# Normalised projection input in a two-layer hybrid trunk: multiplying the last 32 projection tiles by h instead of x, and respacing the work beside them

## The reference, cut to what matters

```python
for each layer:
    x = x + 0.5 * swiglu(rmsnorm(x, norm_ffn1), ffn1_w_in, ffn1_w_out)
    h = rmsnorm(x, norm_mix)
    proj = h @ w_in                       # 6440 columns
    # columns: RWKV group (r, k, v, three small ones), short convolution (b, c, x), SSD group (z, xbc, dt)
    y_rwkv = rwkv7_mix(xs = proj + (previous_row(proj) - proj) * mu, ...)
    y_sc = rmsnorm(b_gate * causal_conv(c_gate * xt), sc_norm)
    y_ssm = mamba2_mix(z, causal_conv(xbc), dt, state, ...)
    x = x + concat([y_rwkv, y_sc, y_ssm]) @ w_out
    x = x + 0.5 * swiglu(rmsnorm(x, norm_ffn2), ffn2_w_in, ffn2_w_out)
```

## Time and profile before

| | before |
|---|---|
| median of 3 runs | 1662.56 us (1658.15 to 1662.92) |
| the profiled execution | 1660.52 us, of which its span 1658.5 us |
| mean granted clock of PE | 0.986 |
| PE busy | 1550.0 us, 93% of the span |
| DVE busy | 1145.6 us, 69% |
| ACT busy | 860.9 us, 52% |
| POOL busy | 264.0 us, 16% |
| share of PE in the chain that ended last | 19% by name; every other engine 2% or less |

### The profile page before, as it was taken

The page is one execution under the profiler, slowest core; times in us unless marked ns, Lnnn a source line. Parts: engine busy times, 40 slices in busy tenths (PEclk is TensorE's granted clock), DMA queues, the critical chain, the costliest instruction groups (busy, mean ns, idle before and its releaser), DMA issues. The chain is left out here.

```text
span 1658.5 us, 41230 instructions
## 1 busy us (share of the span) xinstructions
PE 1550.0 (93%) x17275; PEld 1471.9 (89%) x17275; DVE 1145.6 (69%) x1832; ACT 860.9 (52%) x1521; POOL 264.0 (16%) x259
## 2 busy tenths in 40 slices
PE   7999999989799899999999999998997989899997
PEld 6999999977688789999999999998775878899997
DVE  6565578795798667665575656978768977676654
ACT  5444465767444555444354444657673445554443
POOL 0000003001455531000000000030014554300000
PEclk9999999999899999999999999999998999999999
DMA  7555557471244445555454655654703453465552
GB/s 232 178 168 176 161 157 211 131 210 52 64 127 119 138 150 171 196 174 187 149 186 153 203 166 175 194 157 131 213 1 104 126 166 111 130 199 181 187 176 71
DMA packets 280649, 256.26 MB, mean 155 GB/s; under 512 B 48054, under 2 KB 268700, under 8 KB 280450
## 3 DMA queue, kind: packets, MB, share of 16 engines
q1 hardware_dynamic: 276698, 252.05, 49.3%
q10 hardware_dynamic: 3768, 1.59, 0.4%
HBM read 242.22 MB, written 11.38 MB: 153 GB/s over the span
## 5 line engine op out<-in xcount | busy, mean ns | idle before, releaser
L209 ACT ACTIVATE front_hi<-front_raw 128x1024 fp32r<-128x1024 f32 (+2 forms) x230 | 238.5, 1039 | 257.2 <-PE ps L234 249.7
L216 DVE TENSOR_TENSOR front_lo<-front_raw,front_hi 128x1024 fp32r<-128x1024 f32 (+1 forms) x210 | 252.2, 1201 | 112.5 <-ACT front_hi L209 111.7
L209 ACT ACTIVATE out_hi<-out_raw 128x1024 fp32r<-128x1024 f32 (+1 forms) x168 | 173.2, 1038 | 216.1 <-PE ps L234 202.5
L216 DVE TENSOR_TENSOR out_lo<-out_raw,out_hi 128x1024 fp32r<-128x1024 f32 (+1 forms) x148 | 183.3, 1239 | 109.9 <-ACT out_hi L209 109.3
L232 PE MATMUL ps<-front_h_hi,front_hi 128*128 128x264 f32 (+1 forms) x816 | 241.2, 296 | 8.6 <-DVE front_lo L216 6.7
L234 PE MATMUL ps<-front_h_hi,front_lo 128*128 128x264 f32 (+1 forms) x816 | 233.0, 286 | 0.0
L233 PE MATMUL ps<-front_h_lo,front_hi 128*128 128x264 f32 (+1 forms) x816 | 232.8, 285 | 0.0
L232 PE MATMUL ps<-ffn_h_hi,out_hi 128*128 128x264 f32 x704 | 200.4, 285 | 0.1
L233 PE MATMUL ps<-ffn_h_lo,out_hi 128*128 128x264 f32 x704 | 199.6, 284 | 0.0
L234 PE MATMUL ps<-ffn_h_hi,out_lo 128*128 128x264 f32 x704 | 199.6, 283 | 0.0
L232 PE MATMUL ps<-in_h_hi,front_hi 128*128 128x264 f32 x688 | 197.3, 287 | 0.0
(11 more groups left out here) (410 smaller groups left out, 3861.2 us busy)
## 6 DMA issues: line engine op xcount, KB each, us to landing
front_raw<-in_w_in SPq DMA_DIRECT2D x50, 1024.0 KB, 5.4
out_raw<-in_ffn_w_in SPq DMA_DIRECT2D x44, 1024.0 KB, 5.2
front_raw<-in_ffn_w_in SPq DMA_DIRECT2D x40, 1024.0 KB, 5.3
back_sample_rows<-row_scratch SPq DMA_DIRECT2D x160, 128.0 KB, 3.1
out_raw<-in_w_out SPq DMA_DIRECT2D x16, 1024.0 KB, 5.8
front_raw<-in_ffn_w_out SPq DMA_DIRECT2D x16, 896.0 KB, 5.0
out_raw<-in_ffn_w_out SPq DMA_DIRECT2D x16, 896.0 KB, 4.9
front_raw<-in_ffn_w_out SPq DMA_DIRECT2D x8, 1024.0 KB, 5.4
```

Of the source, the lines that this page charges most:

```text
L209: act.activation(self.hi[n % self.RING][:, 0:k, 0:w], self._raw(n), ACT.Copy).then_inc(self.hi_ready, 1)
L216: eng.tensor_tensor(self.lo[n % self.RING][:, 0:k, 0:w], self._raw(n), self.hi[n % self.RING][:, 0:k, 0:w].bitcast(F32), ALU.subtract).the ...
```

## The change

1. `NORMED = 19`. In slots 10 to 18 x·gain·rs is computed slice by slice: DVE `normed(k)` into `ctmp`, ACT `normed_hi(k)` rounds it into `h_hi`, DVE `normed_lo(k)` the rest into `h_lo`. Tiles 0 to 18 multiply the unnormalised input in other buffers; tiles 19 to 50 multiply h.
2. With h the evictions of tiles 19 to 50 need no `rs`. A `c` tile is one instruction (bank times `u`), a `b` tile multiplies `acc` by the bank (the one large instruction is gone). For the 24 late `rwkv` tiles ACT reads the bank itself, twice, and DVE adds the shifted row from the bank in one instruction, `mix_shifted`, which frees the bank; eviction and shift were two.
3. The keys now come before `b` (slots 23 to 30, `b` 31 to 34).
4. 8 low parts per layer (tiles 14, 16, 18, 20, 22, 24, 44, 46) go from POOL to DVE.
5. Decays at slots 25, 26, 28, 30 (were 25, 25, 26, 26), short convolution at 26, 27, 31, 32 (were 26, 26, 27, 27); transposes of new rows at PE slots 34, 35, 36, one bank after the other (were all at 37), their copies on ACT at 35, 36, 37; mean squares at PE slots 37 and 39; key norms one slot later; logarithm at ACT slot 45 and exponential at 46; bonus at 45, 47, 49, 50.

The core of the diff:

```diff
-                                       ("c", SC0 + 512, 0, 4), ("b", SC0, 0, 4), ("rwkv", 8 * P, 8, 8), ("rwkv", 0, 0, 8),
+                                       ("c", SC0 + 512, 0, 4), ("rwkv", 8 * P, 8, 8), ("b", SC0, 0, 4), ("rwkv", 0, 0, 8),
...
+        H, NORMED = len(tiles), 19
         ws = Stream(st, KT, pieces, halves, raw_ring=3, resident=env.first_raw, made=(env.first_hi, env.first_lo), on_dve={*range(0, base, 2), *range(1, len(halves), 2),
                                                                     *range(base + 4, base + 14, 2), *range(base + 26, base + 43, 2),
-                                                                    *range(base + 48, base + H, 2)})
+                                                                    *range(base + 12, base + H, 2)})
...
+        norm2 = Norm(st, env, "mix", lambda k: env.col("norm_mix", k), A, env.in_hi, env.in_lo, rs, xa, ctmp[:, 0])
...
+                def normed_hi(k):
+                    act.wait_ge(s("normed"), k + 1)
+                    act.activation(h_hi[:, k], ctmp[:, k % 2], ACT.Copy).then_inc(s("normed_hi"), 1)
...
+                    yield 12
+                    normed_hi(1)
                     yield 13
+                    normed_hi(2)
                     act.wait_ge(s("btok_ps"), 1)
                     act.activation(btok[:].rearrange("p c g n -> p (c g n)"), ps[:, A, :], ACT.Copy).then_inc(s("btok_done"), 1)
                     yield 14
+                    normed_hi(3)
                     act.wait_ge(s("smp_conv"), 8)
...
+                        if h in (0, 2):
+                            normed_hi(4 + h)
+                            normed_hi(5 + h)
...
+
+                    for slot, m in ((25, 0), (26, 1), (27, None), (28, 2), (29, None), (30, 3), (32, None), (34, None)):
+                        yield slot
+                        if m is not None:
+                            decay(m)
+                        if slot in (27, 29, 32, 34):
+                            weigh_outer({27: 0, 29: 1, 32: 2, 34: 3}[slot])
...
+                    yield 35
+                    new_rows(0)
+                    yield 36
+                    new_rows(1)
+                    act.wait_ge(evicted, 35)
...
                     act.wait_ge(s("y_gated"), 1)
...
-                        yield slot
+                    for p, slot in enumerate((40, 41, 42, 43, 44, 46, 48, 49)):
                         if p == 5:
+                            yield 45
...
                             act.activation(nrm[:], nrm[:], ACT.Ln, scale=LN_SCALE).then_inc(s("norm_ln"), 1)
                             act.activation(sc_root[:], sc_root[:], ACT.Ln).then_inc(s("norm_ln"), 1)
...
+                            yield 46
                             act.wait_ge(s("norm_ln"), 3)
                             act.activation(nrm[:], nrm[:], ACT.Exp, scale=-0.5, bias=lnb[:, 0:1]).then_inc(s("norm_inv"), 1)
...
+                        yield slot
                         gates(p)
...
+                    if kind == "rwkv" and n >= NORMED:
+                        act.wait_ge(ws.used, base + n + 1)
+                        bank = ps[:, n % 3, 0:N]
+                        act.activation(mix.xs[:, m], bank, ACT.Copy, scale=env.omu[:, m:m + 1]).then_inc(kept, 1)
+                        act.activation(last[:, m], bank[:, T - 1:T + NS], ACT.Copy).then_inc(last_in, 1)
                     ws.split_hi(act, base + n + 4)
...
+                    if kind == "c":
+                        dve.wait_ge(evicted, n)
+                        dve.tensor_tensor(u[:, m, 2:2 + N], u[:, m, 2:2 + N], bank, ALU.mult).then_inc(evicted, 1)
+                        return
+                    if kind == "b":
+                        dve.wait_ge(s("smp_sc"), 5)
+                        dve.wait_ge(s("uconv"), 3 * (m + 1))
+                        dve.tensor_tensor(acc[:, m], acc[:, m], bank, ALU.mult).then_inc(evicted, 1)
+                        return
...
+                def mix_shifted(n, m):
+                    q, bank = order.index(m), ps[:, n % 3, 0:N]
+                    dve.wait_ge(kept, q + 1)
+                    dve.wait_ge(last_in, q + 1)
+                    dve.scalar_tensor_tensor(out=mix.xs[:, m, 1:T], in0=bank[:, 0:T - 1], scalar=env.col("rwkv_mu", m),
+                                             in1=mix.xs[:, m, 1:T], op0=ALU.mult, op1=ALU.add).then_inc(evicted, 1)
...
+                def normed(k):
+                    if k >= 2:
+                        dve.wait_ge(s("normed_lo"), k - 1)
+                    dve.scalar_tensor_tensor(out=ctmp[:, k % 2], in0=env.x[:, k], scalar=env.col("norm_mix", k), in1=rs[:],
+                                             op0=ALU.mult, op1=ALU.mult).then_inc(s("normed"), 1)
+
+                def normed_lo(k):
+                    dve.wait_ge(s("normed_hi"), k + 1)
+                    dve.tensor_tensor(h_lo[:, k], ctmp[:, k % 2], h_hi[:, k].bitcast(F32), ALU.subtract).then_inc(s("normed_lo"), 1)
...
+                    yield 12
+                    normed_lo(0)
+                    normed(2)
+                    yield 13
+                    normed_lo(1)
+                    normed(3)
                     for j in range(4):
                         yield 14 + 2 * j
+                        if j < 2:
+                            for t in (2 + 2 * j, 3 + 2 * j):
+                                normed_lo(t)
+                                normed(t + 2)
+                        if j == 2:
+                            normed_lo(6)
...
+                    yield 33
+                    sample(2)
+                    sample_out(2)
...
+                    late = kind == "rwkv" and n >= NORMED
+                    if n < H and not late:
                         evict(n, kind, m)
...
+                    if late:
+                        mix_shifted(n, m)
...
+                    for i in range(3):
+                        yield 34 + i
+                        if i:
+                            pe.wait_ge(s("rows_done"), i)
+                        else:
+                            pe.wait_ge(s("new_in"), 7)
+                            pe.wait_ge(s("hfin_done"), 1)
+                        for j in range(4):
+                            if i:
...
-                    pe.wait_ge(s("hfin_done"), 1)
+                    pe.wait_ge(s("rows_done"), 3)
...
+                    hi, lo = (env.in_hi, env.in_lo) if n < NORMED else (h_hi, h_lo)
```

## The result

| | before | after |
|---|---|---|
| median | 1662.56 us (1658.15 to 1662.92) | 1689.98 us (1687.52 to 1690.93) |
| ratio to before, 95% interval | | 1.0171 (1.0146 to 1.0195) |
| the profiled execution | 1660.52, span 1658.5 | span 1687.9 |
| mean granted clock of PE | 0.986 | 0.969 |

The kernel is 27.4 us slower, 29.4 between the two profiled spans. The forecast, 1679, had the sign and most of the places, but 1690 lies above its range (1648 to 1688): the loss is 27.4 where 16.4 (from the median) to 19 (from the profiled execution) was forecast.

A forecast was written before the change was run, and what follows sets the result against it. PE, busy 93% of the span, was taken as the bound, its time being work plus waits. Waits 6.7 plus clock 2.8 made 9.5 us a layer, 19 in both: 1660.5 + 19 = 1679.5, forecast as 1679, range 1648 to 1688.

The forecast's parts named there:

- Slots 13, 15, 17: PE waits 3.4 us for b_tok at slot 13; 1.35 and 0.85 more at 15 and 17 for DVE's differences.
- The prices: DVE's new instructions: `normed` and `normed_lo` 0.48 us, upper end 0.76; `mix_shifted` 0.48, between 0.42 and 0.76.
- Slots 31 and 32: PE waits 1.6 us at slot 31 (1.74 before) and 3.1 at 32 (2.47 before), there for banks DVE reads.
- Slot 35: New PE wait of 5.4 us for ACT's copy of new rows, behind sample part 2 and the fourth outer block.
- Slots 36 to 44 and 47: Listed waits at slots 36 to 44 go, minus 4.7 us a layer; new PE wait of 2.9 at slot 47.
- The waits' sum: Lag at the end of a layer's projection, 6.7 us: 5.5 at tile 44 plus 1.2 in slots 45 to 50.
- The term of 1.3 for short waits that no list shows: Slots 36 to 44: a late PE skips waits of under 0.2 us each, gaining 1.3 a layer.
- The clock: PE's lower clock behind the waits of 3.4 and 5.4 us costs 1.4 each, 2.8 a layer; none behind 2.9.
- (a): Rival: DVE's saved work lets sample part 2 start by 346.5, removing later waits: 1648.6 or 1651.4 us; chance 0.26.
- (d): Rival: DVE's busy time doesn't fall in slots 23 to 39, as bank reads are slower; then (c); no own chance.
- (c): Rival, worse: upper `mix_shifted` price, clock dip at slot 47 (1.4 us): 1686.3; with upper `normed` price 1693; chance 0.1.
- Faster by over 0.3%: Whole kernel under the no-change band of 1657.6 to 1667.5 us, by rival (a); chance 0.26.

The follow-up runs named there:

- Experiment 8: The changed kernel with the 8 low parts per layer back on POOL; ratio to the kernel before 1.0350.
- experiment 10: The changed kernel with extra matmuls keeping PE busy ahead of five waits (slots 13, 15, 32, 35, 47); ratio to the kernel before 1.0082.
- experiment 2: The changed kernel with ACT's b_tok copy ahead of h's roundings 1 and 2, and DVE's h work behind the differences; ratio to the kernel before 1.0100.
- experiment 6: The changed kernel with the exponential of the norms back in ACT's slot 45, right behind the logarithm; ratio to the kernel before 1.0173.
- experiment 7: The changed kernel with ACT's gates of p = 5 ahead of the logarithm at slot 45; ratio to the kernel before 1.0151.
- experiment 3: The changed kernel with 30 extra matmuls keeping PE busy ahead of its slot 13 wait for b_tok; ratio to the kernel before 1.0153.
- experiment 12: The changed kernel with b_tok first, h behind the differences, first new rows before the fourth outer block, gates before the logarithm; ratio to the kernel before 1.0019.
- a_gate5: The kernel of experiment 7: the changed kernel with ACT's gates of p = 5 ahead of the logarithm at slot 45; ratio to the kernel before 1.0151.
- experiment 4: The kernel before, with ACT's copy of b_tok also waiting for the eviction of tile 12; ratio to the unedited kernel 1.0070.
- experiment 9: The kernel before, with only the 8 low parts per layer moved from POOL to DVE; ratio to the unedited kernel 1.0000.

## Why the prediction was right and wrong

**Slots 13, 15, 17: right.** The walk through DVE's order had the eviction of tile 12 at 266.0 and `normed(2)` done at 268.5, b_tok at 269.6 and PE's wait at 3.4. In the trace of the changed kernel, DVE, then ACT:

```profile
266.57 0.42 DVE L1200 TENSOR_TENSOR z<-ps,front_norm_rs 128x264 f32<-128x264 f32 x1
...
268.50 0.49 DVE L1212 SCALAR_TENSOR_TENSOR c_gate<-x,cols,front_norm_rs 128x264 f32<-128x264 f32 x1
```

```profile
269.03 0.42 ACT L992 ACTIVATE front_h_hi<-c_gate 128x264 fp32r<-128x264 f32 x1 [2.17 <-DVE c_gate L1212]
269.36 0.58 ACT L1025 ACTIVATE b_tok<-ps 128x512 f32<-128x512 f32 x1
```

Less the 0.54 that this execution starts later, that is within 0.3 us everywhere. Slots 15 and 17 were 1.96 and 0.96 for 1.35 and 0.85.

**The prices: right.** `normed` 0.49, `normed_lo` 0.43, `mix_shifted` 0.48 (mean of 48: 481 ns). The 0.76 was a mean with blocked instructions in it, as supposed (two of them together take 3.07 us at 215.81 in the kernel before, beside POOL's 2.40); with POOL's low parts gone none of the new ones was blocked. Experiment 8 shows what a wrong choice there would have meant.

**Slots 31 and 32: right at 32,** 3.07 for 3.1. At slot 31 it is 0.99 for 1.6, and it is another wait: PE no longer waits for the low part but for DVE to free a bank.

**Slot 35: right in kind, short in size,** 3.34 for 5.4. The chain was the forecast one, sample part 2, outer block, copy:

```profile
356.58 1.22 DVE L1222 TENSOR_TENSOR sample_state<-sample_state,outer 128x1024 f32<-128x1024 f32 x1
```

```profile
360.77 2.17 ACT L1068 ACTIVATE outer<-ps,sample_xdt 128x128 f32<-128x128 f32 x8 [4.87 <-DVE y_short L1232]
...
363.73 0.57 ACT L1088 ACTIVATE sc_new_rows<-ps 18x512 f32<-18x512 f32 x1
```

Counted from PE's passing of slot 32, the copy was forecast done after 16.9 us and was done after 16.8 (347.47 to 364.30). PE took 13.5 us to get there where 11.4 was forecast: the clock had taken the time that the wait would have had. In experiment 10, at full clock, filled and unfilled wait together are 5.7, and in experiment 2 the wait is 4.8.

**Slots 36 to 44 and 47: right.** The waits of 1.64, 1.23, 0.80, 0.48 and 0.56 are gone, and the new one is 2.79 for 2.9. Its reason was only half right: that the exponential had moved didn't matter (experiment 6), that the gates stood behind it did (7).

**The waits' sum: near, and in part by luck,** 6.2 a layer for 6.7. Slots 13, 15 and 17 came 1.0 longer than forecast and the end of the projection 0.6. Slot 35 came 2.1 shorter and slot 31 0.6, and the two small waits of 0.43 and 0.21 went, which the sum had left in. The term of 1.3 for short waits that no list shows had nothing under it: PE idles for 13.9 us in that stretch of the kernel before, and 13.8 of them are the eleven listed waits. (Of these leaves out the 1.23, so the five not shown reach 1.23 and not 0.80.)

**The clock: the step that failed.** The term was 1.4 us each for two stretches, 2.8 a layer. There were four new stretches, behind slots 13, 15, 35 and 47, and the old one behind slot 32 was twice as long; three of the five were twice as long as the one priced. The price was taken from the earlier trace rows, a fall of 3.4 us behind a wait of 2.47; the row was read as the price of any fall. And I had counted none for 2.79, which is longer than the 2.47 of that row, so the row itself spoke against that. Measured, the term is 9.3 a layer for 2.8, the difference of 15.5 and 6.2; filling the waits gave 8.4 and 6.8 of it back. Experiments 3 and 10 show that the cause is PE's idling and that PE's time is really lost. With 9.3 in place of 2.8, the sum would have been 1660.5 + 2 x (6.7 + 9.3) = 1692.5, against 1690.

**The rivals.** (a), the later gain outweighs, fell at the point that it named: sample part 2 didn't start by 346.5 but at 356.6, and the wait at slot 32, which was to go, grew to 3.07. Its premise held: from tile 23 to tile 39 DVE is busy for 58.6 us (309.6 to 384.1) for 62.2 before (300.0 to 373.0). That is 3.6 less where 6.2 had been counted, but it is less, which rules out (d). (c), "worse", gave 1686.3 to 1693 with a chance of 0.1, and 1690 lies within it. Of its three reasons only the clock at slot 47 came, and at about twice its price; the two upper prices didn't, so its number was right by luck. Faster by over 0.3% had 0.26: experiment 12, with four of the places mended, still isn't faster. Waits for DVE stay in it at slots 15 and 16, where DVE works without a break; that no other order would do better isn't shown.

## What to carry to other kernels

A wait of the matrix engine has two prices: its length, and the time at half clock that follows it. Look in the granted clock behind every wait of the trace before pricing one, and count a stretch for each new wait as long as the shortest that had one. Even so the price has a wide range: with the one stretch of 3.4 us in the projection, the three new waits of the forecast that are longer than 2.47 (3.4, 5.4 and 2.9) would have come to 3 x 1.7 = 5.1 us a layer and not to 9.3, as the stretches of twice that length show inside the projection only in other runs. Work that is "moved to the background" still stands in line: what matters is which instruction that the bottleneck waits for it now stands ahead of, here the copy of b_tok, the differences and the copy of the new rows. And where a helper engine works without a break, as DVE in slots 8 to 15 here, look for its new work in the waits whatever the order.

## What was not expected of the hardware

The same wait had different stretches of lower clock behind it, from kernel to kernel and even from layer to layer: 3.66 us at slot 13 was followed by 6.9 us in the changed kernel (0.57 over 8 us, above), 3.67 at the same place in a_gate5 by 3.4:

```profile
273.00:277.00 4.00, 4.00 (x23) 4.00 (x22) 0.33 (x1) 0.80 (x3) 0.00 (x0) 0.57 0.83 258
```

In the second layer of a_gate5 a wait of 3.66 was followed by 6.8 again, and the 2.47 of slot 32 had 3.4 in the kernel before and 6.8 in experiments 4 and 9, whose edits don't touch it. All stretches inside the projection were near 3.4 or 6.9. The 1.54 and 1.22 us at slots 15 and 16 of experiment 2 were followed by none; the same 1.55 in layer 1 of experiment 12 was followed by 3.4. And the 1.96 at slot 15 by one in the changed kernel and by none in experiment 3, where PE had been busy before it. So a price for one wait is uncertain by 1.7 us or more, and part of what single experiments won or lost is this. What decides between the lengths, or whether there is a stretch at all, these runs don't show.
